# Opening of a one-core hybrid trunk step: the first input weights asked for later, and their low-part products moved back

## The reference, cut to what matters

```
mod   = silu(c) @ w_mod + b_mod                # shift, scale, gate; once for context, once for latents
h     = rmsnorm(x, norm_w) * (1 + scale) + shift
proj  = h @ w_in                               # all later branches start from this
```

## Time and profile before

| | us |
|---|---|
| median of 3 runs | 1474.88 (1474.86 to 1475.2) |
| the profiled execution's own time | 1475.35 |
| its span | 1473.5 |
| PE busy | 1451.4 (99% of the span) |
| DVE busy | 1109.2 (75%) |
| ACT busy | 851.0 (58%) |

### The profile page before, as it was taken

The page is one execution under the profiler, slowest core; times in us unless marked ns, Lnnn a source line. Parts: engine busy times, 40 slices in busy tenths (PEclk is TensorE's granted clock), DMA queues, the critical chain, the costliest instruction groups (busy, mean ns, idle before and its releaser), DMA issues.

```text
span 1473.5 us, 29048 instructions
## 1 busy us (share of the span) xinstructions
PE 1451.4 (99%) x11568; PEld 1394.6 (95%) x11568; DVE 1109.2 (75%) x1919; ACT 851.0 (58%) x1789; POOL 432.3 (29%) x366
## 2 busy tenths in 40 slices
PE   8999999999999999999999999999999989999997
PEld 7899999999999999999899999999999989999776
DVE  5798897988889798888858736636637738888864
ACT  6574857567584757657466663763655654453211
POOL 2133322232332322233312212212111255657220
PEclk9999999999999999999999999999999999999999
DMA  9423133333323132433522424421122599746242
GB/s 316 118 69 123 40 78 102 74 109 79 121 62 103 55 89 94 135 109 90 163 58 77 153 78 112 97 83 60 53 71 88 186 275 244 243 150 232 75 153 104
DMA packets 157416, 173.92 MB, mean 118 GB/s; under 512 B 7929, under 2 KB 123490, under 8 KB 157282
## 3 DMA queue, kind: packets, MB, share of 16 engines
q1 hardware_dynamic: 147426, 147.89, 31.9%
q0 software_dynamic: 9568, 23.86, 7.3%
q10 hardware_dynamic: 288, 0.33, 0.1%
HBM read 151.96 MB, written 51.02 MB: 138 GB/s over the span
## 4 chain that ended last, share of the span: by engine, by line
PE 90%; DVE 4%; DMA 2%; issue 2%; SPq 1%; ACT 1%; POOL 1%; POOLq 0%; DVEq 0%; ACTq 0%
PE mb L141 11%; PE mb L143 11%; PE mb L142 11%; PE db L141 10%; PE db L143 9%; PE db L142 9%; PE mb L2512 3%; PE mb L2513 3%; PE mb L2514 3%; PE db L1404 3%; PE db L1376 2%; PE db L1420 2%; PE db L1393 2%; PE db L1414 2%; PE db L1038 2%
## 5 line engine op out<-in xcount | busy, mean ns | idle before, releaser
L141 PE MATMUL db<-h_hi,w_hi 128*128 128x384 f32 x816 | 288.0, 353 | 0.2 <-DVE w_lo L1502 0.2
L142 PE MATMUL db<-h_lo,w_hi 128*128 128x384 f32 x816 | 274.5, 336 | 0.0
L143 PE MATMUL db<-h_hi,w_lo 128*128 128x384 f32 x816 | 274.5, 336 | 0.0
L142 PE MATMUL mb<-h_lo,w_hi 128*128 128x384 f32 x696 | 233.9, 336 | 0.0
L141 PE MATMUL mb<-h_hi,w_hi 128*128 128x384 f32 x696 | 233.9, 336 | 0.0
L143 PE MATMUL mb<-h_hi,w_lo 128*128 128x384 f32 x696 | 233.9, 336 | 0.0
L2205 POOL TENSOR_TENSOR w_lo<-w,w_hi 128x1024 fp32r<-128x1024 f32 x29 | 81.3, 2803 | 310.5 <-ACT w_hi L2262 310.5
L141 PEld LDWEIGHTS db<-h_hi,w_hi 128*128 128x128 f32 x816 | 153.7, 188 | 3.9 <-DVE w_lo L1502 0.7
L142 PEld LDWEIGHTS db<-h_lo,w_hi 128*128 128x128 f32 x816 | 153.9, 189 | 0.0
L143 PEld LDWEIGHTS db<-h_hi,w_lo 128*128 128x128 f32 x816 | 153.4, 188 | 0.0
L2512 PE MATMUL mb<-h_hi,w_hi 128*128 128x288 f32 x448 | 133.3, 298 | 4.6 <-POOL w_lo L2221 4.6
(11 more groups left out here) (383 smaller groups left out, 3406.7 us busy)
## 6 DMA issues: line engine op xcount, KB each, us to landing
w<-in_w_in SPq DMA_DIRECT2D x48, 512.0 KB, 4.2
d_dt<-decay_rows SPq DMA_DIRECT2D x16, 576.0 KB, 6.1
d_qg<-decay_rows SPq DMA_DIRECT2D x16, 512.0 KB, 4.3
weight_sums<-in_w_proj_a POOLq DMA_DIRECT2D x8, 1024.0 KB, 10.3
weight_sums<-in_w_proj_b POOLq DMA_DIRECT2D x8, 1024.0 KB, 10.3
w<-in_w_gate SPq DMA_DIRECT2D x16, 512.0 KB, 4.1
branch_a<-d_kq SPq DMA_DIRECT2D x8, 576.0 KB, 3.2
branch_b<-l_z SPq DMA_DIRECT2D x8, 576.0 KB, 2.8
```

Of the source, the lines that this page charges most:

```text
L141: pe.matmul(out, hi, rhi, start=(k == 0), stop=False)
L142: pe.matmul(out, hi, rlo, start=False, stop=False)
L143: return pe.matmul(out, lo, rhi, start=False, stop=(last and stop))
```

## The change

Three moves. On SP, `load(0)` stands behind the requests for modulation blocks 2 and 3 and no longer ahead of them. On ACT, `high(0)` stands behind the copy of the last turned tile of x and no longer ahead of it. On PE, the products of k tiles 0 and 1 with the low weights leave `first_high` and become `first_weights_low(0)` (behind `first_high(1)`) and `first_weights_low(1)` (behind block 7); the wait ahead of `first_high(0)` is for `w_hi` instead of `w_lo`, and that for `w_lo` stands ahead of the moved products. No instruction of work is added or removed.

```diff
@@ -439,9 +439,9 @@
             mod_load(1)
-            load(0)
             mod_load(2)
             mod_load(3)
+            load(0)
@@ -767,11 +767,11 @@
             normalise(NT - 1)
-            high(0)
             act.wait_ge(S["x_t"], NT)
...
             ins.then_inc(S["x_e"], 1)
+            high(0)
@@ -1086,6 +1086,13 @@
                     pe.matmul(bank[2 + g][:, 0:GW], whi[:, 0, k, :], R.hhi[:, k, ts], start=(k == 0), stop=False)
+                    if k > 1:
+                        pe.matmul(bank[2 + g][:, 0:GW], wlo[:, 0, k, :], R.hhi[:, k, ts], start=False, stop=False)
+
+            def first_weights_low(k):
+                low_done(pe, 0)
+                for g in range(NG):
+                    ts = slice(g * GW, (g + 1) * GW)
                     pe.matmul(bank[2 + g][:, 0:GW], wlo[:, 0, k, :], R.hhi[:, k, ts], start=False, stop=False)
@@ -1135,14 +1142,16 @@
             idle(8)
-            low_done(pe, 0)
+            pe.wait_ge(S["w_hi"], 1)
             first_high(0)
             modulate(4)
             modulate(5)
             first_low(0)
             first_high(1)
+            first_weights_low(0)
             modulate(6)
             modulate(7)
+            first_weights_low(1)
             pe.wait_ge(S["x_e"], NT)
```

## The result

| | before | after |
|---|---|---|
| median of 22 runs each, in turn | 1474.87 us (1473.21 to 1477.1) | 1477.33 us (1475.14 to 1479.86) |
| ratio, 95% interval | | 1.0017 [1.0011, 1.0024] |
| the profiled execution's own time | 1475.35 | 1476.17 |
| its span | 1473.5 | 1474.3 |

The changed kernel is slower by 0.17% (2.5 us), and no difference at all is outside the interval. The forecast was 1475.3 with a range to 1476.4, so the prediction was wrong. The loss is a little under the 0.2% (2.95 us) named as the bound of what can be told.

The account below looks back on a forecast made before the run. PE, busy 99% of the span, was taken as the bound. Terms -0.88 + 0.03 + 0.72 + 0.52 = +0.39 us on the 1474.88 median gave 1475.3 us, range 1473.9 to 1476.4.

Parts of the forecast that it names:

- Part 1: Request moved on SP: block 3 lands at 24.6, PE starts it at 25.43 instead of 26.31, gaining 0.88 us.
- Part 2: High part moved on ACT: rounding waits for weights at 26.3, ends at 27.4; k tile 0 rows start 0.85 us earlier.
- ACT starts them 0.85 us earlier than before: ACT's rows of k tile 0 follow gain and shift, forecast at 27.38 instead of 28.26.
- Part 3: POOL's low part takes 2.36 us from 27.5 to 29.9, before the first product needing it at 31.7.
- covered by 1.8 us: POOL's low part ends at 29.9, 1.8 us ahead of PE's first product that needs it, at 31.7.
- the sum: Opening up to turn_columns(1): -0.88 block 3, +0.03 ACT's rounding, +0.72 wait for block 7, +0.52 three products, giving +0.39 us.
- my rivals: Block 7 doesn't hold PE (0.20), gain arrives whole (0.12), weights land late (0.12), clock falls (0.03): 1474.6, 1474.0, 1476.6, 1476.8.
- Part 4: Three products behind block 7: PE waits for block 7 until 33.5, then turn_columns(1) comes at 35.21, 0.39 us later.
- The wait of 0.72 us for block 7: PE wants block 7 at 32.8, but its second half lands at 33.5, so PE waits about 0.7 us.
- The 0.52 us for three products: Products moved between block 7 and turn_columns(1), priced at 0.17 us each from six run between 32.06 and 33.20.
- rival 4: PE's new 0.7 us wait at 33 us halves the clock for 3 us, costing 1.5 us: 1476.8, chance 0.03.
- I find nothing that would soak up a shift: Behind turn_columns(1), PE's work and order are unchanged, so a shift of 0.4 us reaches the end.

## Why the prediction was wrong, point by point

**Block 3 and the request (Part 1): right.** Block 3 was found landed, and `turn_columns(0)` gained 0.87 us of the 0.88 forecast. The weights' landing, 8.9 us behind their issue at 16.93, is 25.83, against 26.3 forecast.

**ACT's rounding (Part 2): its start was near, what follows was not.** Line 648 ran at 25.88, behind the copy; 26.3 was forecast. "ACT starts them 0.85 us earlier than before" failed: ACT's rows started at 29.50, 1.24 us later than before, since gain was not made at 27.38 but at 29.38.

**POOL's low part (Part 3): the step that failed.** POOL's length was right and its time near (2.34 us from 27.02; forecast 2.36 from 27.5), and "covered by 1.8 us" was right in this: nobody waited for `w_lo`. But I asked only who waits for its result, and not what else runs beside it. It holds DVE's gain product, 2.28 us instead of 0.17, and the sum has no term for that. Shown from two sides: POOL's subtraction late in the kernel before, with no other edit, makes the hold and a loss (1.0013 [1.0004, 1.0022]); the subtraction taken off POOL in the changed kernel, together with the products back from behind block 7, removes both (1.0003 [0.9994, 1.0012]). None of my rivals had it. In the terms of the sum, the first profile has -0.88 for block 3, 0 for ACT's rounding, +2.11 for the hold, 0 for block 7, +0.88 for the products and +1.12 for the clock: 3.23 us, where 0.39 was forecast.

The trace of before had the sign, outside the stretch that I read. POOL and DVE in the kernel before, at 60 and at 72 us:

```profile
60.26 2.39 POOL L550 TENSOR_TENSOR w_lo<-w,w_hi 128x1024 fp32r<-128x1024 f32 x1 [25.44 <-ACT w_hi L648]
...
60.99 0.37 DVE L1623 TENSOR_TENSOR d_qg<-db,dt_bias 128x72 f32<-128x72 f32 x2 [1.06 <-PE db L1182]
61.40 1.33 DVE L1629 TENSOR_SCALAR d_qg<-d_qg 128x144 f32<-128x144 f32 x1
...
66.50 0.23 DVE L1646 TENSOR_SCALAR d_qg<-d_qg 128x144 f32<-128x144 f32 x1
...
71.92 2.40 POOL L550 TENSOR_TENSOR w_lo<-w,w_hi 128x1024 fp32r<-128x1024 f32 x1 [9.28 <-ACT w_hi L648]
...
72.82 2.73 DVE L1448 SCALAR_TENSOR_TENSOR d_q<-padded_rows,par,d_q 128x1155 f32<-128x1155 f32 x1
```

A TENSOR_SCALAR on 128x144 takes 1.33 us beside POOL and 0.23 later, and the instruction at 72.82 takes 2.73 us where its two followers take 1.42 each. The two that read PSUM (`db`) at 60.99 pass in 0.37 together. Nothing on PE waited for these, so no view of waits named them. Not every instruction on SBUF is held: at 177 us in the kernel before, four transposes by DVE run beside the same subtraction, and neither side is lengthened (0.69 to 0.71 us for each of the four):

```profile
177.06 2.91 DVE L1736 STREAM_TRANSPOSE w<-d_u 32x288 f32<-32x288 f32 x4
177.20 2.39 POOL L550 TENSOR_TENSOR w_lo<-w,w_hi 128x1024 fp32r<-128x1024 f32 x1
```

**The products behind block 7 (Part 4): two terms mis-sized.** The wait of 0.72 us for block 7 did not come: its landing was as forecast (its second half, issued at 26.9, landed 6.6 us later, at 33.5), but PE wanted it only at 36.0, and at 34.10 with the products moved alone. No run brought PE to block 7 as early as the 32.8 of my sum, so whether it would have waited there stays open. The 0.52 us for three products measured 0.85 to 0.88, since a price from the middle of a run of equal instructions leaves out what lies at its ends: with the products moved alone, 0.11 us more passes ahead of them, 0.20 more from their start to the next group, and 0.02 more in `gates(0)`.

**The clock (rival 4, chance 0.03): it happened in one profile of the changed kernel, and cost 1.12 us as worked out above.** In the second profile of it, and in the experiments where PE waited 0.8 to 1.8 us at the same place, the granted clock stayed at 1.00. So the wait alone doesn't decide, and what does stays open.

**What reached the end.** "I find nothing that would soak up a shift" holds only in part. Set beside the first profile, ACT's instructions of the same number start 3.25 us later at 50 to 130 us, 2.8 at 320, 2.0 from 655 to 1187 and 0.8 from 1207 on. The last step is PE's wait for POOL's `w_lo` there, 3.3 us in the changed kernel and 4.6 before. But the medians lie 2.5 us apart, and another profile need not end so. The same stretch shows one reason: behind that wait the clock is low, and not for equally long. The kernel before, then the changed kernel again (columns as in the earlier trace rows):

```profile
1205.00:1212.00 7.00, 7.00 (x54) 7.00 (x54) 4.13 (x3) 3.81 (x9) 4.65 (x4) 1.00 0.97 289
...
1205.00:1212.00 7.00, 7.00 (x44) 7.00 (x44) 4.69 (x4) 4.33 (x10) 4.93 (x4) 0.79 0.64 220
```

With VectorE doing the subtraction the wait is 4.9 us and the granted clock 0.81 here, and PE's instructions of the same number, 0.07 us ahead of before from 900 to 1187 us, are 1.44 behind it at 1207. Single profiles thus differ by over 1 us at a place that no edit touches, and no run shows whether the edits change how often that happens. The excess of the medians over what the openings show stays open: the products moved alone cost 1.6 us by the medians and 0.85 in the opening, within an interval of 0.4 to 3 us.

**The spread.** Three runs of before lay within 0.34 us and I took 0.3 us for what executions differ by; 22 runs spread over 3.9 us. The interval of the ratio is what the 0.2% bound should have been weighed against: a loss of 2.5 us is seen well with 22 runs.

## What to carry to other kernels

Before a GpSimd instruction is moved, lay its new place over VectorE's timeline and not only over the waits for its result: beside a VectorE instruction that it holds, on the path, it costs up to its own length. Look for it as a known instruction of unusual length, since the waits don't list it, and compare the same instruction elsewhere in the trace. Where a product moves from a place where PE waits on another engine's rows to one behind that wait, count it whole, and with the change of kind at its two ends.

## What the runs showed of the hardware that was not expected

- VectorE's SBUF instructions were held by one GpSimd TENSOR_TENSOR (128x1024 float32, 2.34 to 2.44 us) in these overlaps: TENSOR_TENSOR of 128x4 (2.28, 2.04, 1.44, 1.41 us, 0.17 free), TENSOR_SCALAR (2.49 and 2.47 us, 0.34 and 0.41 free), SCALAR_TENSOR_TENSOR (2.73, 1.42 free). Two TENSOR_TENSOR that read PSUM and four STREAM_TRANSPOSE on SBUF (0.7 us each) were not. A subtraction that came behind a running VectorE instruction took 3.42 us instead of 2.41.
- The subtraction takes 1.22 us on VectorE and 2.35 on GpSimd.
- Behind a like idle time of TensorE (1.65, 1.41, 1.68 and 1.82 us), the granted clock fell once to 0.50 and stayed at 1.00 three times.
